# Bringing the whole fifth input-projection slot ahead of convolution tiles 2 and 3

## The reference, cut to what matters

```
hn = rmsnorm(h) ; u = hn @ w_in                  # w_in: 1024 x 1536
pool_out = pool(u[:, :512])                      # 4 groups of 128 channels, windows 2, 4, 8, 16
v = u[:, 512:1024] * sigmoid(u[:, 1024:1536])    # GLU
y = causal depthwise conv of v, width 31, + bias # 4 tiles of 128 channels
y = silu(layernorm(y)) ; conv_out = y @ pw_w
h = h + concat(pool_out, conv_out) @ w_out
pool(x): per group, mean over the window minus x, then @ w_grp, * scale
```

## Time and profile before

| | us |
|---|---|
| median of 3 runs | 1544.91 (1544.33 to 1546.05) |
| the profiled execution | 1547.83 |
| its span | 1546.0 |
| TensorE (PE) busy | 1486.1, 96% of the span |
| VectorE (DVE) busy | 1205.3 |
| ScalarE (ACT) busy | 963.6 |
| GpSimd (POOL) busy | 181.0 |
| mean granted TensorE clock | 0.98 |

### The profile page before, as it was taken

The page is one execution under the profiler, slowest core; times in us unless marked ns, Lnnn a source line. Parts: engine busy times, 40 slices in busy tenths (PEclk is TensorE's granted clock), DMA queues, the critical chain, the costliest instruction groups (busy, mean ns, idle before and its releaser), DMA issues.

```text
span 1546.0 us, 20888 instructions
## 1 busy us (share of the span) xinstructions
PE 1486.1 (96%) x7639; PEld 1298.9 (84%) x7639; DVE 1205.3 (78%) x1001; ACT 963.6 (62%) x812; POOL 181.0 (12%) x216
## 2 busy tenths in 40 slices
PE   7979999999987999999999999999999999999995
PEld 7869999999976997788888888888888888888884
DVE  4776765544477568888888888888888888888888
ACT  3555333423254457777777777777777777777773
POOL 1035300001103404740000000000000000000002
PEclk8989999999998999999999999999999999999998
DMA  6363899344146439999999999999999999999994
GB/s 196 97 207 105 268 321 270 111 130 157 55 102 202 134 130 367 398 389 390 376 388 374 370 391 360 388 384 361 381 392 365 385 382 370 385 375 374 385 382 136
DMA packets 249678, 453.40 MB, mean 293 GB/s; under 512 B 9605, under 2 KB 99781, under 8 KB 249631
## 3 DMA queue, kind: packets, MB, share of 16 engines
q1 hardware_dynamic: 245056, 442.20, 80.6%
q0 software_dynamic: 2960, 9.73, 2.0%
q10 hardware_dynamic: 1615, 0.85, 0.2%
HBM read 426.38 MB, written 26.37 MB: 293 GB/s over the span
## 4 chain that ended last, share of the span: by engine, by line
issue 55%; PE 5%; POOL 5%; DVE 2%; DMA 2%; ACT 1%; POOLq 0%; DVEq 0%; ACTq 0%
PE ps L1747 1%; PE ps L1748 1%; PE ps L1749 1%; POOL xg L775 1%; POOL h L799 1%; DMA xg<-og,row_i 1%; DMA og<-obuf,out_row_i 0%; DMA last_row<-last_pos 0%; DVE scratch L1255 0%; DVE y L1257 0%; DMA h<-last_row 0%; POOL win_sum L708 0%; POOL key L787 0%; PE ps L2104 0%; POOL pick L795 0%
## 5 line engine op out<-in xcount | busy, mean ns | idle before, releaser
L531 DVE TENSOR_TENSOR w_lo<-raw,w_hi 128x2048 fp32r<-128x2048 f32 x336 | 764.4, 2290 | 117.5 <-ACT w_hi L526 116.3
L526 ACT ACTIVATE w_hi<-raw 128x2048 fp32r<-128x2048 f32 x334 | 639.5, 1915 | 123.6 <-PE ps L1749 122.2
L1749 PE MATMUL ps<-w_hi,xg_lo 128*128 128x512 f32 x896 | 351.6, 392 | 0.0
L1747 PE MATMUL ps<-w_hi,xg_hi 128*128 128x512 f32 x896 | 351.5, 392 | 0.0
L1748 PE MATMUL ps<-w_lo,xg_hi 128*128 128x512 f32 x896 | 350.5, 391 | 0.0
L1747 PE MATMUL ps<-x_hi,w_hi 128*128 128x336 f32 x580 | 192.8, 332 | 13.7 <-DVE w_lo L511 5.1
L1748 PEld LDWEIGHTS ps<-w_lo,xg_hi 128*128 128x128 f32 x896 | 168.4, 188 | 37.0
L1749 PEld LDWEIGHTS ps<-w_hi,xg_lo 128*128 128x128 f32 x896 | 168.5, 188 | 36.4
L1747 PEld LDWEIGHTS ps<-w_hi,xg_hi 128*128 128x128 f32 x896 | 168.5, 188 | 36.1 <-DVE w_lo L531 0.2
L1748 PE MATMUL ps<-x_lo,w_hi 128*128 128x336 f32 x580 | 188.5, 325 | 0.0
L1749 PE MATMUL ps<-x_hi,w_lo 128*128 128x336 f32 x580 | 187.7, 324 | 0.0
(11 more groups left out here) (288 smaller groups left out, 1708.4 us busy)
## 6 DMA issues: line engine op xcount, KB each, us to landing
raw<-in_moe_w_gate_dram SPq DMA_DIRECT2D x112, 1024.0 KB, 7.3
raw<-in_moe_w_up_dram SPq DMA_DIRECT2D x112, 1024.0 KB, 7.7
raw<-in_moe_w_down_dram SPq DMA_DIRECT2D x112, 1024.0 KB, 7.5
raw<-in_w_in_dram SPq DMA_DIRECT2D x11, 1024.0 KB, 5.1
raw<-in_ffn_w_gate_dram SPq DMA_DIRECT2D x11, 1024.0 KB, 6.1
raw<-in_ffn_w_up_dram SPq DMA_DIRECT2D x11, 1024.0 KB, 6.4
raw<-in_w_out_dram SPq DMA_DIRECT2D x8, 1024.0 KB, 6.8
obuf<-ones SPq DMA_DIRECT2D x15, 512.0 KB, 8.0
```

What stands on the lines that cost most here:

```text
L526: nc.scalar.activation(hi, r, ACT.Copy).then_inc(hi_done, 1)
L531: nc.vector.tensor_tensor(lo, r, hi.bitcast(F32), ALU.subtract).then_inc(lo_done, 1)
L1747: nc.tensor.matmul(out, a_hi, b_hi, start=start, stop=False)
L1749: return nc.tensor.matmul(out, a_lo, b_hi, start=False, stop=stop)
```

## The change

The work is the same; its order changes in five places, alike in both layers. In the plan and on TensorE both halves of the fifth slot and the fold of tile 1 come ahead of the parts of tiles 2 and 3. On ScalarE the hi split of the fifth slot moves between the two pairs of row copies of tile 0; the bias copy of tile 1 comes ahead of the rows of tile 2; that of tile 2 and then the hi split of the sixth slot and the bias copy of tile 3 follow the rows of tile 3, and `pooled_high` of the first pooled group comes behind them. On VectorE `pool_in(4, 0)` comes ahead of `turned_low(2)` and `turned_low(3)`, and `pool_in(4, 1)` directly behind these, ahead of most of the samples. (`part_rows` has a new argument, the pairs to copy; `pooled_high` is only defined earlier.)

```diff
@@ -117,10 +117,10 @@
         plan_parts(l, 0)
         plan(("win", l, 2 * WIN_ORDER[3] + 1))
         plan_parts(l, 1)
-        plan(("conv", l, 0), ("win", l, 2 * WIN_ORDER[4]))
+        plan(("conv", l, 0), *[("win", l, 2 * WIN_ORDER[4] + i) for i in (0, 1)], ("conv", l, 1))
         plan_parts(l, 2)
         plan_parts(l, 3)
-        plan(("conv", l, 1), ("win", l, 2 * WIN_ORDER[4] + 1), ("conv", l, 2), ("conv", l, 3))
+        plan(("conv", l, 2), ("conv", l, 3))
         plan(*[("win", l, g) for g in POOL_ORDER[2:]], *[("pool", l, g) for g in POOL_ORDER[:2]])
         plan(*[("pw", l, m) for m in range(KC)], *[("pool", l, g) for g in POOL_ORDER[2:]])
         for m in range(KD):
@@ -930,12 +930,17 @@
                         act.wait_ge(mm_done, GROUP[("part", l, c - 2, NB - 1)] + 1)
                     nc.scalar.activation(turned[:, c % 2, 0], x_turned(l, c), ACT.Copy).then_inc(e_hi_done, 1)
 
-                def part_rows(c):
-
-                    if ("even", l, c) in GROUP:
+                def pooled_high(g):
+                    q = POOL_ORDER.index(g)
+                    act.wait_ge(pooled, NG * l + q + 1)
+                    nc.scalar.activation(pooled_at(g)[0], y_pool[:, g, :], ACT.Copy).then_inc(pooled_hi, 1)
+
+                def part_rows(c, pairs=(0, 2)):
+
+                    if pairs[0] == 0 and ("even", l, c) in GROUP:
                         act.wait_ge(evac, GROUP[("even", l, c)])
                         act.sem_inc(evac, 1)
-                    for g in range(0, NB, 2):
+                    for g in pairs:
                         at = GROUP[("part", l, c, g)]
                         act.wait_ge(mm_done, at + 2)
                         for q in range(NB):
@@ -955,31 +960,27 @@
                                          ).then_inc(tap_hi_done, 1)
                 turned_high(0)
                 turned_high(1)
-                part_rows(0)
+                part_rows(0, (0,))
                 split_to(b + W_AT[4])
+                part_rows(0, (2,))
                 gated(1)
                 part_rows(1)
                 conv_with_bias(0)
                 turned_high(2)
                 turned_high(3)
+                conv_with_bias(1)
                 part_rows(2)
                 part_rows(3)
-                conv_with_bias(1)
-
-                def pooled_high(g):
-                    q = POOL_ORDER.index(g)
-                    act.wait_ge(pooled, NG * l + q + 1)
-                    nc.scalar.activation(pooled_at(g)[0], y_pool[:, g, :], ACT.Copy).then_inc(pooled_hi, 1)
+                conv_with_bias(2)
 
                 def m_high(name, k, scale):
                     act.wait_ge(mm_done, GROUP[name] + 1)
                     nc.scalar.activation(m_hi[:, k, :], ps[:, GROUP[name] % MM_BANKS, 0:T], ACT.Copy, scale=scale
                                          ).then_inc(m_hi_done, 1)
 
+                split_to(b + W_AT[5])
+                conv_with_bias(3)
                 pooled_high(POOL_ORDER[0])
-                split_to(b + W_AT[5])
-                conv_with_bias(2)
-                conv_with_bias(3)
                 split_to(b + S_POOL_W)
                 pooled_high(POOL_ORDER[1])
                 split_to(b + S_PW)
@@ -1352,17 +1353,16 @@
                 split_to(b + W_AT[4])
                 tap_blocks(2)
                 tap_blocks(3)
-                turned_low(2)
-                turned_low(3)
-                conv_samples(1, (0,))
                 dve.wait_ge(evac, GROUP[("conv", l, 0)] + 1)
                 pool_in(4, 0)
                 split_to(b + D_AT[3])
+                conv_samples(1, (0,))
+                turned_low(2)
+                turned_low(3)
+                pool_in(4, 1)
                 conv_samples(1, (1,))
                 conv_samples(2)
                 conv_samples(3)
-                dve.wait_ge(evac, GROUP[("conv", l, 1)] + 1)
-                pool_in(4, 1)
 
                 def pooled_low(g):
 
@@ -1934,10 +1934,10 @@
                 conv_parts(1)
                 conv_fold(0)
                 w_in_slot(4, (0,))
+                w_in_slot(4, (1,))
+                conv_fold(1)
                 conv_parts(2)
                 conv_parts(3)
-                conv_fold(1)
-                w_in_slot(4, (1,))
                 conv_fold(2)
                 conv_fold(3)
 
```

## The result

The changed kernel takes 1524.74 us (median of 4 runs, 1522.97 to 1527.42), the kernel before 1544.81 beside it (4 runs, 1544.33 to 1546.05): a ratio of 0.987, interval 0.9852 to 0.9889, or 20.1 us. The forecast was 1529 in a range of 1523 to 1537. The profiled execution after took 1527.42, its span is 1525.6, its mean granted clock 0.986.

What follows compares the result with a forecast made beforehand. The bound was an ordering in the mixer stage: the late copy `pool_in(4, 1)`, GpSimd's group, then squares and spread. 8 us per layer, 16 in all, gave 1531.8 from 1547.83, or 1529 as median; range 1523 to 1537.

Steps and rivals of the forecast that it cites:

- Head, +0.5: Tile 0 rows, with the fifth slot's split between them: gated rows near 68.1 instead of 67.6, cost 0.5 us.
- The sum: Both layers' gain, 2 x 8 = 16 us, off the profiled 1547.83: 1531.8; the median 2.9 lower, so 1529.
- Slot 5, rows, fold: Fifth slot done at 79 us, last rows 94.5, tile 3's fold 98; costs 0.3 (bounds -1.2 and +1.5).
- GpSimd's price, 0.8: VectorE slowed beside GpSimd's pooled groups: 0.8 us ahead of `pool_in(4, 1)`, bounds 0 and 2.6.
- Squares and sums: LayerNorm: first square 102.4 instead of 108.18 us, sums ended 106.6, spread 109.9 instead of 118.89.
- The two levels: Spread earlier by 9.0 us per layer if the clock holds, 6.7 if the 21 matmuls are slow.
- One sign of being wrong: TensorE between sums and spread: a granted clock of 0.5 under the 21 matmuls would show the forecast wrong.
- The first: TensorE's clock falls back after new pauses: gain 4.7 to 6.7 us per layer, 1531.5 to 1535.5; chance 0.22.
- The second: Tiles 2 and 3 bound, `pool_in(4, 1)` 2-3 us late: gain 5-6 us per layer, 1533-1535; chance 0.12.
- The third: TensorE starved from 64 us stays slow: spread near 124.8, 5.9 us late per layer, 1557; chance 0.05.
- The fourth: Later stages, set by the weight stream, absorb the gain: 1543 to 1546 us; chance 0.06.

Runs made afterwards that it cites:

- e3_squares_first: Kernel before, ScalarE's squares moved ahead of the second pooled group and pw split, VectorE's variance factors ahead of pw's low half: 1533.13 us.
- e4_copy_late: Changed kernel with `pool_in(4, 1)` moved behind all samples on VectorE: 1554.20 us, 1.0058 of the kernel before.
- e1: Changed kernel with the fifth slot's hi split back behind all eight row copies of tile 0: 1529.25 us.
- e10: Changed kernel with the fifth slot's hi split behind all tile 0 rows and TensorE's idle ahead of the slot filled by ten small matmuls: 1524.70 us.
- the second profile: The changed kernel run once more with no edit: 1525.29 us, 0.9867 of the kernel before.
- e5_keep_busy: Changed kernel with 12 matmuls that nobody reads between the folds of tiles 2 and 3: 1524.09 us.

## Why the prediction was right, and where its sum was off

The mechanism stood as written: ScalarE's wait for the pooled group is gone, the first square comes 7 us nearer to the first row copy (42.6 us behind it, 49.9 before), e3_squares_first shows that the wait for that group held the squares, and e4_copy_late what the copy's place is worth. Times from the first row copy of tile 0 (58.32 in the earlier trace rows, 55.26 after), layer 0:

| step | predicted | measured |
|---|---|---|
| slot 5 begins | 12.2 | 11.7 |
| its 48 matmuls | 8.5 | 7.65 |
| `pool_in(4, 1)` ended | 24.5 | 23.8 |
| last rows ended | 36.2 | 35.0 |
| TensorE's idle before fold 3 | 3.5 | 3.3 |
| fold 3 | 3.4 | 3.55 |
| first centring | 42.6 | 41.3 |
| first square | 44.1 | 42.6 |
| sums ended | 48.3 | 46.3 |
| spread | 51.6 to 55.9 | 49.6, 52.3 |

- **Head, +0.5: it was nothing.** The gated rows end 9.2 us after the first row copy in both kernels, the low split of the slot begins 9.4 us after it in both (I had 9.93), and slot 5 begins at 11.74, as before (11.76). TensorE's third part of tile 1 waits 1.54 us where I had 2. What I did not work out is the other side of that new pause: the one ahead of the slot fell from 2.69 to 0.70 us, and the slot runs at full clock. e1 and e10 price this at 4 to 4.5 us of the median for both layers. The sum had 8.5 us for the slot, for a slow start that then did not come; it took 7.65.
- **Slot 5, rows, fold: right** to within 0.9 us each; the slot and the rows were shorter than counted, the fold 0.15 longer. The slow clock in fold 3, for a pause shorter than 5 us, came as written, in every profile without filler (2.8 to 4.0 us, against 2.07 with filler).
- **GpSimd's price, 0.8: low, inside its bounds.** The two turned lows took 3.90 us against the 2.6 counted, so 1.3. GpSimd was itself slower: its second group ended 35.3 us after the first row copy, not 33.7. ScalarE asks for it at 40.4, so that costs nothing.
- **Squares and sums: right, by 2 us too late.** 1.2 us of this came with the rows. Sums took 2.43 (2.6 counted as the upper end). The spread came 10.9 and 7.9 us nearer to the first row copy (8.2 and 10.4 in the second profile). The forecast had 9.0, or 6.7 with the 21 matmuls slow, and took 8: mean measured 9.35. The two levels that it named are both seen, each 1.2 to 1.9 us better than I had them. One sign of being wrong that it named, a granted clock of 0.5 under the 21 matmuls, did come, in one layer of each profile. So 8 was the right choice by luck as much as by reason: it was taken because the clock was expected to hold, and half of the time it did not, while each level came out better.
- **The sum.** 2 x 8 = 16 against 20.1: of the missing 4.1, 2.7 are in D, and most of that (1.2 a layer) was there by the last rows; the other 1.4 lies outside it, in starts that differ by chance (first row copies from 55.2 to 58.3 in the profiles), and is not resolved further.
- **The rivals.** The first is half true: behind the sums the clock falls back in one layer of two (gain 7.9 and 8.2 in D there, where I had 6.7 at most), so it is inside the gain, not instead of it. The second (copy 2 to 3 us late) did not come; e4 shows that its mechanism is real and as I priced it, a microsecond for each: ended 13.8 us later (37.6 against 23.8 behind the first row copy), it costs 29 us for both layers. The third would have needed fold 3 to end at 103; it ended at 94.1. The fourth is out: the 18.7 us of D are all there at the end of the kernel, so no later stage absorbed them.

No version tried beats the changed kernel by what can be told: e5_keep_busy and e10_back_filled are level with it.

## What to carry to other kernels

Where banks are given back in a fixed order, a copy's place in its engine's queue matters by who waits behind its bank, not by who reads it: follow the counter before you move a group up. Before an order is changed for one late item, list what stands in front of it in that engine's queue; letting the squares past the pooled group and its neighbour brought 60% here. And count each pause that an edit makes, cuts or moves on TensorE: one of 2.5 us cut into one of 0.7 and one of 1.5 to 1.9 was worth some 4 us by the medians, a fifth of the whole gain, with the work behind it starting no earlier.

## What the runs showed of the hardware that I had not expected

- The dip of the clock moved on rather than going away. In the changed kernel the last fold was slow, and the 21 matmuls behind the 24 one-column passes in one layer of two; with the pause ahead of the fold filled (e5_keep_busy) the fold was fast and the 21 were slow in both layers, at nearly the same median.
- In e5_keep_busy the clock fell from 1.00 (98 to 100 us) to 0.57 (100 to 102 us) behind the 24 passes of one column, with the engine busy for 2.00 of 2.00 us in both stretches.
- In the kernel before, the granted clock still read 1.00 in the idle from 104 to 108 us, 0.59 from 108 to 108.8 and 0.50 under the sums: the pause was paid for behind it.
- Two executions of one kernel differ in where the clock falls: D was 49.63 and 52.40 in one, 52.33 and 49.90 in the other, with the same sum of about 102.
- A VectorE instruction on two SBUF inputs took longer beside GpSimd: a sample product 1.87 us against 1.19, and two turned lows 3.90 us together, where one alone took 1.37.
